# Queries and keys of a transformer block computed by token, rotated along rows and transposed, in place of computed by feature

## The reference

```python
xn = rms_norm(x, attn_norm)
h = xn @ w_in        # split: cq 384, ckv 256, kr 32, dq 512, dk 512, dv 512, gq 384, gk 128, gv 128
q_a = (rms_norm(cq) @ mla_w_uq)    # 6 heads of 96: 64 plain features, 32 rotated
kv  = (rms_norm(ckv) @ mla_w_ukv)  # 6 heads of 64 key features and 64 value features
k_a = concat(k_nope, kr for all 6 heads)
q_a, k_a = rms_norm over 96, times a gain; rotary embedding on the last 32
q_b, k_b = 4 heads x 2 halves of 64: rms_norm over 64, gain, rotary embedding
q_c, k_c = 6 query heads, 2 key heads of 64: rms_norm, gain, rotary embedding by row and column
o = softmax(q k^T * scale) v    # "dif" pairs subtract two softmaxes
x = x + concat(o_a, o_b, o_c) @ w_o
x = x + (silu(gate) * up) @ w_down
```

## Time and profile before

| what | value |
|---|---|
| median of three executions | 1784.71 us |
| profiled execution, its own time | 1787.21 us |
| its span | 1785.3 us |
| TensorE busy (matmul / weight load) | 98% / 94% of the span |
| VectorE, ScalarE, GpSimd busy | 67%, 51%, 5% |
| mean granted clock of TensorE | 0.991 of full |
| weight DMA | 272.14 MB, 44.9% of 16 engines' span |

### The profile page before, as it was taken

How to read it: one execution, slowest core, us unless ns; L and a number is a source line. 1 busy time by engine, 2 the same in 40 slices (tenths; PEclk the granted TensorE clock), 3 DMA queues, 4 the chain that set the end, 5 groups by cost and what they waited for, 6 DMA issues and landing times.

```text
span 1785.3 us, 32432 instructions
## 1 busy us (share of the span) xinstructions
PE 1758.4 (98%) x13954; PEld 1683.5 (94%) x13954; DVE 1204.8 (67%) x1678; ACT 906.5 (51%) x1276; POOL 93.8 (5%) x60
## 2 busy tenths in 40 slices
PE   9999999999999999999999999999999999999997
PEld 9887999999878999999999999999989999899997
DVE  5777676646676776457766857985466758769863
ACT  5466544444556444363444665554434545655542
POOL 2000000020000000030000110000200000010000
PEclk9999999999999999999999999999999999999999
DMA  7321555544213554464434444654455345435551
GB/s 273 109 72 47 184 200 185 182 161 147 88 48 110 197 182 153 158 247 169 157 125 160 159 148 135 219 179 159 155 167 174 107 149 190 146 125 193 196 174 41
DMA packets 52416, 275.26 MB, mean 154 GB/s; under 512 B 5937, under 2 KB 6321, under 8 KB 52145
## 3 DMA queue, kind: packets, MB, share of 16 engines
q1 hardware_dynamic: 52128, 272.14, 44.9%
q10 hardware_dynamic: 144, 1.05, 0.2%
HBM read 272.12 MB, written 1.05 MB: 153 GB/s over the span
## 4 chain that ended last, share of the span: by engine, by line
PE 89%; DVE 8%; ACT 2%; issue 1%; ACTq 0%; DVEq 0%
PE bank L755 19%; PE bank L758 18%; PE bank L757 18%; PE scores L755 3%; PE scores L757 3%; PE scores L758 3%; PE heads L755 2%; PE heads L757 2%; PE heads L758 2%; DVE weights_lo L627 1%; PE bank L1220 1%; PE scores L1079 1%; PE bank L764 1%; DVE x_lo L880 1%; PE bank L766 1%
## 5 line engine op out<-in xcount | busy, mean ns | idle before, releaser
L627 DVE TENSOR_TENSOR weights_lo<-raw,weights_hi 128x1536 fp32r<-128x1536 f32 (+3 forms) x344 | 586.6, 1723 | 258.7 <-ACT weights_hi L616 258.1
L616 ACT ACTIVATE weights_hi<-raw 128x1536 fp32r<-128x1536 f32 (+3 forms) x352 | 500.9, 1442 | 225.6 <-PE bank L758 92.5
L755 PE MATMUL bank<-x_hi,weights_lo 128*128 128x256 f32 (+1 forms) x1808 | 521.2, 288 | 0.4 <-DVE weights_lo L627 0.4
L758 PE MATMUL bank<-x_hi,weights_hi 128*128 128x256 f32 (+1 forms) x1808 | 512.6, 284 | 0.0
L757 PE MATMUL bank<-x_lo,weights_hi 128*128 128x256 f32 (+1 forms) x1808 | 512.5, 283 | 0.0
L755 PEld LDWEIGHTS bank<-x_hi,weights_lo 128*128 128x128 f32 (+1 forms) x1808 | 345.7, 191 | 7.9 <-issue 4.8
L757 PEld LDWEIGHTS bank<-x_lo,weights_hi 128*128 128x128 f32 (+1 forms) x1808 | 345.7, 191 | 2.6 <-issue 2.0
L758 PEld LDWEIGHTS bank<-x_hi,weights_hi 128*128 128x128 f32 (+1 forms) x1808 | 345.8, 191 | 0.0
L755 PE MATMUL bank<-hidden_hi,weights_lo 128*128 128x256 f32 x704 | 196.9, 280 | 0.0
L757 PE MATMUL bank<-hidden_lo,weights_hi 128*128 128x256 f32 x704 | 196.9, 280 | 0.0
L758 PE MATMUL bank<-hidden_hi,weights_hi 128*128 128x256 f32 x704 | 196.9, 280 | 0.0
(11 more groups left out here) (373 smaller groups left out, 3215.1 us busy)
## 6 DMA issues: line engine op xcount, KB each, us to landing
raw<-in_w_b SPq DMA_DIRECT2D x194, 768.0 KB, 4.5
raw<-in_w_a SPq DMA_DIRECT2D x122, 768.0 KB, 4.5
raw<-in_w_a SPq DMA_DIRECT2D x14, 512.0 KB, 3.6
raw<-in_w_b SPq DMA_DIRECT2D x10, 512.0 KB, 4.0
raw<-in_w_b SPq DMA_DIRECT2D x2, 752.0 KB, 4.3
raw<-in_w_a SPq DMA_DIRECT2D x2, 736.0 KB, 4.2
raw<-in_w_b SPq DMA_DIRECT2D x2, 720.0 KB, 5.2
raw<-in_w_a SPq DMA_DIRECT2D x2, 704.0 KB, 4.3
```

What stands on the lines that cost most here:

```text
L616: nc.scalar.activation(whi[c % SPLIT][:, 0:n], raw[c % RAW][:, 0:n], ACT.Copy).then_inc(*s.mark("weights_hi", c))
L627: nc.vector.tensor_tensor(wlo[c % SPLIT][:, 0:n], raw[c % RAW][:, 0:n], whi[c % SPLIT][:, 0:n].bitcast(F32), ALU.subtract).then_inc(*s.mar ...
L755: ins = nc.tensor.matmul(dst, wl, xh, start=start, stop=False, skip_group_check=skip)
L758: ins = nc.tensor.matmul(dst, wh, xh, start=False, stop=stop, skip_group_check=skip)
```

## The change

All of it is in the first block.

- The twelve query and key jobs are now by token: the bank holds two token tiles of 256 (or 192) columns. ScalarE squares it. VectorE does the rotation out of the bank along rows, with tables that hold gain times cosine and gain times signed sine (`vector_tables`, twelve instructions a layer, from rows of gains that a new DMA brings), sums the squares by head with TENSOR_REDUCE and makes the mean. The bank is free only when VectorE has made the mean (`qk_mean`), and no longer when ScalarE has squared.
- `turn` and `spread_keys` are gone. In their place are `rope` (VectorE), `scale` (VectorE: keys times head factors) and `flip` (TensorE: transposes into a ring bank; ScalarE: copy to QK).
- `kr` and `gv` are one job `kv` by token of 160 columns. The `uk` jobs take keys and values together (256 columns); `uv0` and `uv1` are gone.
- `dq`, `dk0`, `g0`, `g1` and `kv` may use all six banks. So `pair_in 0` now waits for the last users of the two score banks, and the first heads for that of the heads bank.

```diff
-    job("dq0", "w_in", "x", cols(C_DQ, 2), full)
-    job("kr", "w_in", "x", [[(C_KR - NOPE, MLA_QK)]], full)
+    job("dq0", "w_in", "x", [[(C_DQ, T)]], full, feature=False)
+    job("kv", "w_in", "x", [[(C_KR, ROPE), (C_GV, GQA_KV * GQA_D)]], full, feature=False)
...
+    for i in range(3):
+        job(f"uk{i}", "mla_w_ukv", "ckv", [[(i * T, T)]], even(2), feature=False)
...
-                    ("spread_keys", "dk0"), ("spread_keys", "g1"), ("pair_in", 0), ("turn", "dk1"), ("roots", "late"), ("lambda", 0)]
+                    ("job", "dk1"), ("flip", "dk0"), ("scale", "gk"), ("flip", "g1"), ("rope", "dq1"),
+                    ("pair_in", 0), ("rope", "dk1"), ("roots", "late"), ("lambda", 0)]
...
             if name[:2] in ("dq", "dk", "uq", "uk") or name in ("g0", "g1"):
-                return ("qk_sq", name)
+                return ("qk_mean", name)
...
             if i < PAIRS:
                 if i >= 1:
                     pe.wait_ge(*s.at(l, "map_exp", 2 * i - 1))
+                else:
+                    for c in range(2):
+                        pe.wait_ge(*ring_free[BANKS + c])
...
+        def tensor_flip(pl, pe, l, name):
...
+            for w, o, src in flip_parts(name):
+                ins = nc.tensor.transpose(ps[0:w, o:o + P], src, ident)
+            ins.then_inc(*s.mark("filled", f"flip_{name}"))
...
+        def vector_rope(pl, dve, l, name):
...
+            q, t1, t2 = by_head(ps[:, :], 4), by_head(st, 4), by_head(T2[:, :], 4)
+            for a, b, tab in ([(0, 2, "gq"), (2, 4, "gk")] if name == "g1" else [(0, 4, fam)]):
+                nc.vector.tensor_tensor(t1[:, :, a:b, :], q[:, :, a:b, :], table(0, tab, b - a), ALU.mult)
+                for half in range(2):
+                    ins = vector_turned(t2, q, tab, a, b, 4, half)
+            ins.then_inc(*s.mark("qk_t2", name))
+            dve.wait_ge(*s.at(l, "qk_t2", name))
+            nc.vector.tensor_tensor(st, st, T2[:, :], ALU.add).then_inc(*s.mark("qk_sum", name))
+            nc.vector.tensor_reduce(HROOT[:, i, :], heads_of(sq_of(i), DIF_D), AX.X, ALU.add).then_inc(*s.mark("head_sums", name))
+            dve.wait_ge(*s.at(l, "head_sums", name))
+            nc.vector.scalar_tensor_tensor(out=HROOT[:, i, :], in0=HROOT[:, i, :], scalar=1.0 / DIF_D, in1=NEPS[:, :], op0=ALU.mult, op1=ALU.add)              .then_inc(*s.mark("qk_mean", name))
```

More of the change, by code:

```diff
@@ L953, in transformer @@
[L953 to L957 removed]
+        order_a += [("job", "cq0"), ("job", "cq1"), ("adds", "n1"), ("job", "ckv"), ("mean", "n1"), ("tables", 0), ("job", "dq0"), ("factor", "n1"), ("job", "kv")]
@@ new lines, in transformer @@
+        inside = {2: [("rope", "uk0")], 3: [("rope", "uk1"), ("rope", "uk2")], 4: [("rope", "uq0"), ("rope", "uq1")],
+                  5: [("rope", "uq2"), ("flip", "uq1")], 6: [(what, f"uk{i}") for i in range(3) for what in ("scale", "flip")],
+                  7: [("dif_spread", 0)], 12: [("root_table", "o"), ("job", "o3")]}
+        after = {0: [("job", "dv0"), ("flip", "dq1"), ("scale", "dk1"), ("flip", "dk1")], 1: [("job", "dv1"), ("flip", "gk"), ("job", "uk0")],
+                 2: [("job", "uk1"), ("job", "uk2")], 3: [("job", "uq0"), ("job", "uq1")], 4: [("job", "uq2"), ("flip", "uq0")],
+                 5: [("flip", "uq2"), ("dif_sum", 0), ("roots", "mla")], 7: [("dif_out", 0)],
```

433 lines of the change are left out of this document (257 added, 176 removed).

## The result

The changed kernel takes 1803.87 us (median of 4 runs, 1802.93 to 1806.35) against 1785.2 us for the kernel before on the same chip (1782.41 to 1786.24): ratio 1.0109, 95% interval 1.0092 to 1.0127. It is slower by 1.1%; forecast were 1775 us and a range of 1761 to 1790. The profiled execution has a span of 1802.4 us, 17.1 more than before; forecast were 10 less.

The account below looks back on a forecast made before the run. TensorE bounded the kernel before; after the change VectorE's queue would return some 40 of 49.6 us as waits. Fronts -2.8 and pair stretches -7.2 make -10 us, from 1784.7 to 1775; range 1761 to 1790.

Parts of the forecast that it names:

- VectorE's queue takes the gain away: Main forecast, first-block layers: of 49.6 us taken from TensorE, some 40 return as waits for VectorE; chance 0.57.
- ropes dear: Rival, VectorE's strided ropes: at 20% more per rope, scale and sum, 11 us in all, 1785 us, no change; chance 0.15.
- TensorE stays the bound: Rival, first block: the full 49.6 us gives 1735 us, half of it 1760; chance 0.13 for this or near it.
- The flip of `dk1`: Pair stretch: TensorE waits 3 us before this flip, which needs VectorE's scaling of `dk1`.
- busy above 90% in the fronts: Sign of being right: VectorE busy above 90% in the stretches before the first scores.
- 5 to 6 7.4: Pair stretch: the pipeline step between the turns of pairs 4 and 5 takes 7.4 us.
- the clock 2.5 us a layer: Pair stretches: clock drops from TensorE's idling cost 2.5 us a layer; a clock under 0.88 would show it wrong.
- after pair 7 the steps are as before: Behind the pair stretch: steps after pair 7 stay as before and chain-bound.
- Most low stretches fall into waits: Pair stretches: the reason given for allowing only 2.5 us a layer for low clock.
- I add 1 us for ScalarE's split: Front: 1 us added to VectorE's 27.5 us queue, as ScalarE's split now stands behind a root.
- step 6 of 10.8 us: Pair stretch, step 6 to 7: pair 6's exponentials behind three key copies and a table load, 10.8 us against 7.9 before.
- the clock falls and stays: slower: Rival, pair stretches: a clock like 0.80 costs some 10 us a layer more, 1795 us; gain gone from 5; chance 0.15.

## Why the prediction was wrong

**Right: VectorE's queue takes the gain away.** The durations were those forecast: a rope of `dk` 2.8 us, `g0` 2.9, `g1` 3.2. The second layer's front:

```profile
446.89 0.69 DVE L1355 TENSOR_TENSOR qk<-heads,rope_tables 128x512 f32<-128x512 f32 x1
447.50 0.74 DVE L1299 TENSOR_TENSOR t<-heads,rope_tables 128x256 f32<-128x256 f32 x2
448.27 0.69 DVE L1360 TENSOR_TENSOR qk<-qk,t 128x512 f32<-128x512 f32 x1
448.88 0.68 DVE L1361 TENSOR_REDUCE head_root<-pair_squares 128x8 f32<-128x512 f32 x1
449.60 0.17 DVE L1363 SCALAR_TENSOR_TENSOR head_root<-head_root,scaled_eps 128x8 f32<-128x8 f32 x1
449.68 3.42 DVE L645 TENSOR_TENSOR weights_lo<-raw,weights_hi 128x1536 fp32r<-128x1536 f32 x2
```

From 446.89 to 449.68 are 2.79 us. Strided reads out of PSUM with a broadcast table cost by the element like any others, 0.69 us for 512; the rival *ropes dear* is out, and so is *TensorE stays the bound*. The first scores wait 4.74 us in the first layer (forecast: more than 4) and 4.75 in the second (4), lambda 4.65 (4 to 5), and exponentials of pair 6 stand behind the key copies. The flip of `dk1` waits 1.22, not 3: `dv0` in front of it ran partly at half clock. One sign of being right failed: VectorE was to be busy above 90% in the fronts, and it is for 39.62 of 50.94 and 35.30 of 46.22 us, 78 and 76%. The queue is serial only from the latents on (50.37 in the first layer).

**Failed: the step from pair 4's turn to pair 5's, "5 to 6 7.4".** At full clock it takes an estimated 9.1 us in both layers (10.5 measured in the second, less the 1.4 us of overrun shown above): 3.3 us for both. I had counted scores, maxima, exponentials and normalising. The chain is another: ScalarE makes the exponentials of pair 5, two copies of turned probabilities and then the squares of pair 3's heads; TensorE's dif sums wait for these and stand ahead of the turn. Moving them away brought the step from 11.2 and 12.2 to 8.2 and 8.0 us. It could have been read from the trace before the change: its step took 10.36 us, with a wait for the same squares.

```profile
133.26 1.03 PE L1071 MATMUL turned<-const,probs 128*128 128x128 f32 x8
...
141.84 0.35 PE L1235 MATMUL bank<-const,squares 128*128 128x2 f32 x2 [0.54 <-ACT squares L1157]
143.62 1.07 PE L1071 MATMUL turned<-const,probs 128*128 128x128 f32 x8
```

**Failed, the largest term: "the clock 2.5 us a layer".** Zero matmuls in the waits won 12.6 us in all; 5 were allowed. By the traces 12.8: 7.4 (2.6 + 4.8) in the pair stretches, whose clock was under the 0.88 that I had named as the sign of this, and 5.4 in the step behind them, of which I had said "after pair 7 the steps are as before". Their own overrun ahead of the dif sums hid another 4.5 us (1.4 and 3.1), so an estimate of the clock's price is 17.3 us, 12.3 more than allowed. "Most low stretches fall into waits" was the error: they don't end with the wait; scores stand first behind it, at half clock, and VectorE's maxima, the exponentials and the next turn stand behind the scores.

**Failed, small: "I add 1 us for ScalarE's split".** Both fronts came 1.6 us late. ScalarE squares the rotated keys of `kv` ahead of its split of the chunk for `g1`, and the squares wait for VectorE; so VectorE's own split waits 1.17 us in the first layer and 1.18 in the second:

```profile
445.10 1.76 DVE L645 TENSOR_TENSOR weights_lo<-raw,weights_hi 128x1536 fp32r<-128x1536 f32 x1 [1.18 <-ACT weights_hi L634]
```

**Failed: step 6 of 10.8 us** was 11.6 at full clock, 1.6 us for both layers; the flips moved behind the exponentials gave 6 us, so its mechanism was right.

**Not in the forecast at all: 5.5 us outside.** In each layer `o3`'s job now gets the heads bank from the ring and waits 0.94 us for its last reader; 2.1 us for both layers with what stands around it. The other 3.4 us stand where the change only moves tiles. Padding the tiles back gave 2.1 of them by the traces, and 1.8 by the times, about their uncertainty. Where the last 1.2 us come from stays open.

The sum: 12.3 us of clock beyond what was allowed, 5.9 of chain in the pair stretches (3.3 and 1.6 above, 1.0 in the other steps), 3.3 in the fronts, 5.5 outside are the 27 us. How the first two share their 18.2 us rests on the estimate above; without it they are 7.8 and 10.4. The rival *the clock falls and stays: slower* named the right place and the right sign at 0.15, and its mechanism is the largest part of the miss: 6.1 us a layer beyond the 2.5 by the estimate (3.9 by what the zero matmuls won), where it had set its point of decision at 5. Alone it would have left the time at 1787, close to the kernel before. What made the kernel 1.1% slower is that with it the other terms, all on one side, were each read too low. A chain summed from its shortest parts has errors of one sign only, and my range took in none.

## What to carry to other kernels

When work goes from the bounding engine to one in whose queue the next stage waits, sum that queue; but take the length of each pipeline step from the same step in the trace before, and go below it only for a link whose removal you can name. Count what stands behind each new wait at half clock, the step after included, and try a few zero matmuls in the waits: here 12.6 us with the right number, and 29 us lost with about twice as many. Look in the trace whether they end before what the next instruction waits for; ahead of the dif sums they didn't. And before comparing two layouts, look at the matmul rows of a stretch that the change doesn't touch: a shift of 32 or 64 bytes is worth as much as the change.

## What was not expected of the hardware

- The place of SBUF tiles changes the pace of float32 matmuls: rows of the down jobs of 282, 280 and 276 or 277 ns at 0, 32 and 64 bytes past a multiple of 128, with weight tiles at 0; 7 us of the kernel before, 13 of the changed one. In the stretches that the change doesn't touch it is 9.6 and 12.2.
- While GpSimd subtracts two SBUF tiles, VectorE's instructions with two SBUF inputs stand until it ends (0.69 to 3.22 us, 0.17 to 2.74); those that read PSUM and reductions of one SBUF input don't.
- A plain float32 matmul of 128 columns counts twice (two records 0.112 us apart), a transpose once; both hold the granted clock equally (0.989 and 0.991).
